# Modulation's sums over partitions: from one block of one-column products in the next mixer to ones matmuls inside the feed-forwards

## What is computed

```python
def second_block(x, c, ...):
    c_act = jax.nn.silu(c)
    mod = c_act @ ada_w[i] + ada_b[i]
    sh1, sc1, g1, sh2, sc2, g2 = [m[:, None, :] for m in jnp.split(mod, N_MOD, axis=-1)]
    h = rms_norm(x, mix_pre_g[i]) * (1.0 + sc1) + sh1
    y = hybrid_mixer(h, ...)
    x = x + g1 * rms_norm(y, mix_post_g[i])
    h = rms_norm(x, ffn_pre_g[i]) * (1.0 + sc2) + sh2
    y = swiglu_ffn(h, w_ffn_in[i], w_ffn_out[i])
    x = x + g2 * rms_norm(y, ffn_post_g[i])
```

## Time and profile before

| | |
|---|---|
| three runs | 1231.95, 1237.13 and 1238.58 us, median 1237.13 |
| the profiled execution | 1230.79 us, its span 1229.0 us |
| granted TensorE clock, mean | 0.983 |
| TensorE (PE) busy | 1163.5 us, 95% of the span |
| VectorE busy | 845.0 us, 69% |
| ScalarE busy | 614.6 us, 50% |
| the ada sums (lines 1554, 1557) | 24 and 168 operations, 8.3 and 81.5 us |
| the two old blocks on TensorE | 455.91 and 887.66 us after the span's start, 48 records each |

### The profile page before, as it was taken

How to read it: one execution, slowest core, us unless ns; L and a number is a source line. 1 busy time by engine, 2 the same in 40 slices (tenths; PEclk the granted TensorE clock), 3 DMA queues, 4 the chain that set the end, 5 groups by cost and what they waited for, 6 DMA issues and landing times.

```text
span 1229.0 us, 21102 instructions
## 1 busy us (share of the span) xinstructions
PE 1163.5 (95%) x9014; PEld 1127.7 (92%) x9014; DVE 845.0 (69%) x1270; ACT 614.6 (50%) x738; POOL 0.2 (0%) x4
## 2 busy tenths in 40 slices
PE   5899999999999999999999999999897988999996
PEld 5799899999999988998999999999897888999996
DVE  6995575777776788955657777767898647644443
ACT  7675336453434355753464534344577365434433
POOL 0000000000000000000000000000000000000000
PEclk9999999999999999999999999999998998999998
DMA  9455342756687653463427566876444221655501
GB/s 345 146 166 179 130 138 78 234 194 218 229 281 275 202 197 112 150 197 113 138 76 236 195 218 228 282 274 209 152 155 154 70 92 65 222 172 188 190 35 35
DMA packets 177614, 214.15 MB, mean 174 GB/s; under 512 B 3696, under 2 KB 160752, under 8 KB 177520
## 3 DMA queue, kind: packets, MB, share of 16 engines
q1 hardware_dynamic: 176800, 211.86, 52.3%
q10 hardware_dynamic: 720, 0.94, 0.2%
HBM read 211.74 MB, written 1.05 MB: 173 GB/s over the span
## 4 chain that ended last, share of the span: by engine, by line
PE 69%; DVE 19%; ACT 7%; issue 3%; DMA 1%; SPq 0%; DVEq 0%; ACTq 0%
PE stream L494 15%; PE stream L496 15%; PE stream L495 15%; DVE w_lo L1345 7%; PE steps L494 5%; PE steps L496 4%; PE steps L495 4%; ACT w_hi L914 3%; PE steps L829 2%; PE steps L684 1%; PE stream L705 1%; DMA raw<-in_w_in 1%; DVE conv_acc L1864 1%; ACT probs L914 1%; DVE score L1482 1%
## 5 line engine op out<-in xcount | busy, mean ns | idle before, releaser
L1345 DVE TENSOR_TENSOR w_lo<-raw,w_hi 128x2048 fp32r<-128x2048 f32 (+2 forms) x178 | 402.5, 2265 | 232.9 <-ACT w_hi L914 232.0
L914 ACT ACTIVATE w_hi<-raw 128x2048 fp32r<-128x2048 f32 (+2 forms) x178 | 336.5, 1893 | 336.6 <-PE stream L496 298.6
L494 PE MATMUL stream<-h_hi,w_hi 128*128 128x256 f32 x1576 | 451.2, 286 | 7.5 <-DVE h_lo L1737 3.8
L496 PE MATMUL stream<-h_hi,w_lo 128*128 128x256 f32 x1576 | 447.7, 284 | 0.0
L495 PE MATMUL stream<-h_lo,w_hi 128*128 128x256 f32 x1576 | 447.7, 284 | 0.0
L494 PEld LDWEIGHTS stream<-h_hi,w_hi 128*128 128x128 f32 x1576 | 303.9, 193 | 10.2 <-DVE w_lo L1345 5.2
L495 PEld LDWEIGHTS stream<-h_lo,w_hi 128*128 128x128 f32 x1576 | 303.9, 193 | 0.6 <-issue 0.5
L496 PEld LDWEIGHTS stream<-h_hi,w_lo 128*128 128x128 f32 x1576 | 303.7, 193 | 0.0
L494 PE MATMUL steps<-gu_hi,w_hi 128*128 128x256 f32 x528 | 149.8, 284 | 1.9 <-DVE gu_lo L1605 1.9
L496 PE MATMUL steps<-gu_hi,w_lo 128*128 128x256 f32 x528 | 149.7, 283 | 0.0
L495 PE MATMUL steps<-gu_lo,w_hi 128*128 128x256 f32 x528 | 149.7, 283 | 0.0
(11 more groups left out here) (289 smaller groups left out, 1635.0 us busy)
## 6 DMA issues: line engine op xcount, KB each, us to landing
raw<-in_w_ffn_in SPq DMA_DIRECT2D x66, 1024.0 KB, 5.2
raw<-in_w_in SPq DMA_DIRECT2D x54, 1024.0 KB, 5.8
raw<-in_w_ffn_out SPq DMA_DIRECT2D x33, 1024.0 KB, 7.1
ada_raw<-in_ada_w SPq DMA_DIRECT2D x24, 1024.0 KB, 5.4
raw<-in_w_out SPq DMA_DIRECT2D x8, 1024.0 KB, 5.1
raw<-in_w_proj_attn SPq DMA_DIRECT2D x8, 512.0 KB, 3.6
raw<-in_w_proj_hgrn SPq DMA_DIRECT2D x8, 512.0 KB, 4.6
raw<-in_w_o SPq DMA_DIRECT2D x4, 1024.0 KB, 5.0
```

Source lines behind the costliest of these rows:

```text
L494: pe.matmul(dst, w_h, x_h, start=start, stop=False, skip_group_check=True)
L496: return pe.matmul(dst, w_l, x_h, start=False, stop=stop, skip_group_check=True)
L914: return act.activation(out_, in_, func, **kw)
L1345: tt(wl[m % SPL][:, 0:n], raw[m % RAW][:, 0:n], wh[m % SPL][:, 0:n].bitcast(F32), ALU.subtract)\
```

## The change

The sum over partitions is taken by a matmul with a 128x128 matrix of ones as weights and the sums moving. ada_sum is split: ScalarE rounds a high part ada_h, VectorE subtracts the low part ada_l, both one step after the sum; another step later, behind up(i) and ahead of down(i - 1), TensorE multiplies ones with the high and the low part of 256 sums into bank S[3]. Every row of that bank then holds the 256 results. VectorE picks the diagonal: a multiply by the identity with a reduction (tensor_tensor_reduce) of each 128x128, giving one column of mod, then adds the bias. That is done behind gu_lo of the same step. Sums are made in steps 1 to 8 only, two each in steps 3, 5, 6 and 8, and their loads are due up to five units earlier; the eight groups follow in steps 3 to 10. ones is rounded to fp32r by ScalarE at the start of each of the two feed-forwards. ada_sum, ada_h and ada_l have four slots each. Bank S[3] is taken out of the round of gate and up units in these feed-forwards, which shifts the banks of all later units. Both old blocks, and VectorE's adds and gain operations beside them, are gone from the mixer and the second block; the gains are made at the end of the last group.

```diff
 ADA_LAYER = 12
-ADA_STEP = (1, 2, 3, 4, 5, 5, 6, 7, 8, 9, 9, 10)
+ADA_STEP = (1, 2, 3, 3, 4, 5, 5, 6, 6, 7, 8, 8)
+ADA_STEPS = sorted(set(ADA_STEP))
+ADA_GROUPS = [[j for j in range(ADA_LAYER) if ADA_STEP[j] == i] for i in ADA_STEPS]
 ADA_AFTER = {UFF[b] + n: ADA_LAYER * b + j for b in range(2)
-             for j, n in enumerate((3, 6, 11, 14, 17, 20, 23, 24, 26, 29, 32, 35))}
+             for j, n in enumerate((3, 6, 11, 14, 17, 19, 21, 24, 25, 27, 28, 30))}
...
     for u in UNITS:
+        if u[0] == "gate" and u[1] < 2 and u[2] == 0:
+            free_at.append(last[3])
+            last[3] = ("mod", len(ADA_GROUPS) * (u[1] + 1))
...
             for _ in range(2 if u[0] in ("merge", "tw") or shifted(u) else 1):
+                if bank == 3 and u[0] in ("gate", "up") and u[1] < 2:
+                    bank = 0
                 banks.append(bank)
...
-    ada_sum = at("ada_sum", [P, ADA_LAYER, UC], F32, 128)
+    ada_sum = at("ada_sum", [P, 4, UC], F32, 128)
+    ada_h = at("ada_sum_hi", [P, 4, UC], F32R, 132)
+    ada_l = at("ada_sum_lo", [P, 4, UC], F32R, 136)
+    mod_term = at("modulation_term", [P, 4, P], F32, 140)
...
+    ones_r = at("ones_r", [P, P], F32R, 142)
...
-        def modulation(b):
-
-            if b == 0:
-                for e, c in BANKS[ada_unit][1]:
-                    pe.wait_ge(evac[e], c)
-            pe.wait_ge(ada_summed, ADA_LAYER * (b + 1))
-            for j in range(2 * ADA_LAYER):
-                mm = pe.matmul(ada_bank[b][:, j:j + 1], ada_sum[:, j // 2, P * (j % 2):P * (j % 2) + P], ones[:, 0:1],
-                               start=True, stop=True)
-            mm.then_inc(ada_done, 1)
+        def modulation(b, g):
+
+            if g == 0:
+                pe.wait_ge(*ones_rounded.at(b))
+                pe.wait_ge(evac[MOD_FREE[b][0]], MOD_FREE[b][1])
+            if b or g:
+                pe.wait_ge(ada_read.sem, len(ADA_GROUPS) * b + g)
+            for n, j in enumerate(ADA_GROUPS[g]):
+                pe.wait_ge(ada_lo, ADA_LAYER * b + j + 1)
+                dst = S[3][:, UC * n:UC * n + UC]
+                pe.matmul(dst, ones_r, ada_h[:, j % 4, :], start=True, stop=False)
+                pe.matmul(dst, ones_r, ada_l[:, j % 4, :], start=False, stop=True).then_inc(ada_done, 1)
...
             stream(3)
-            stream(3 * FS - 5, normed(2 * b + 1))
+            stream(2, normed(2 * b + 1))
+            for i in range(2, FS):
+                if i - 2 in ADA_STEPS:
+                    modulation(b, ADA_STEPS.index(i - 2))
+                stream(3 if i < FS - 1 else 2)
...
             stream(1)
-            if b == 1:
-                modulation(0)
...
-        modulation(1)
         stream(7, normed(4))
...
         def feed_forward(b):
+            if b < 2:
+                f(ones_r, ones, ACT.Copy).then_inc(*lane.mark(ones_rounded))
...
+                if b < 2 and i - 1 in ADA_STEPS:
+                    for j in ADA_GROUPS[ADA_STEPS.index(i - 1)]:
+                        n = ADA_LAYER * b + j + 1
+                        act.wait_ge(ada_summed, n)
+                        if n > 4:
+                            act.wait_ge(ada_done, n - 4)
+                        f(ada_h[:, j % 4, :], ada_sum[:, j % 4, :], ACT.Copy).then_inc(ada_hi, 1)
...
+        def summed_low(b, g):
+
+            for j in ADA_GROUPS[g]:
+                n = ADA_LAYER * b + j + 1
+                dve.wait_ge(ada_hi, n)
+                if n > 4:
+                    dve.wait_ge(ada_done, n - 4)
+                tt(ada_l[:, j % 4, :], ada_sum[:, j % 4, :], ada_h[:, j % 4, :].bitcast(F32), ALU.subtract).then_inc(ada_lo, 1)
+                lane.last = (ada_lo, n)
...
+        def modulation(b, g):
+
+            first = 2 * (ADA_LAYER * b + ADA_GROUPS[g][0])
+            n = 2 * len(ADA_GROUPS[g])
+            dve.wait_ge(ada_done, ADA_LAYER * b + ADA_GROUPS[g][-1] + 1)
+            for c in range(n):
+                dve.tensor_tensor_reduce(mod_term[:, c, :], S[3][:, P * c:P * c + P], ident, 1.0, 0.0, ALU.mult,
+                                         ALU.add, flat_mod[:, first + c:first + c + 1]).then_inc(*lane.step())
+            dve.wait_ge(*lane.last)
+            cols = flat_mod[:, first:first + n]
+            tt(cols, cols, pc("ada_b", first, n), ALU.add).then_inc(*lane.mark(ada_read))
+
+        def gains(b):
+
+            dve.wait_ge(*lane.last)
...
+            ts_(gain[:, 1, :], mod[:, 4, :], 1.0, None, ALU.add).then_inc(*lane.step())
+            tt(gain[:, 2, :], mod[:, 2, :], pc("mix_post", 0, 8), ALU.mult).then_inc(*lane.step())
+            tt(gain[:, 3, :], mod[:, 5, :], pc("ffn_post", 0, 8), ALU.mult).then_inc(*lane.step())
+            dve.wait_ge(*lane.last)
+            tt(gain[:, 1, :], gain[:, 1, :], pc("ffn_pre", 0, 8), ALU.mult).then_inc(*lane.mark(gains_set))
...
+                if b < 2 and i - 2 in ADA_STEPS:
+                    modulation(b, ADA_STEPS.index(i - 2))
+                    if i - 2 == ADA_STEPS[-1]:
+                        gains(b)
+                if b < 2 and i - 1 in ADA_STEPS:
+                    summed_low(b, ADA_STEPS.index(i - 1))
                 for j in range(ADA_LAYER if b < 2 else 0):
                     if ADA_STEP[j] == i:
                         sum_ada(ADA_LAYER * b + j)
...
-                modulation(0)
-                dve.wait_ge(*lane.last)
-                ts_(gain[:, 0, :], mod[:, 1, :], 1.0, None, ALU.add).then_inc(*lane.step())
-                dve.wait_ge(*lane.last)
-                tt(gain[:, 0, :], gain[:, 0, :], pc("mix_pre", 0, 8), ALU.mult).then_inc(*lane.mark(gains_set))
...
         conv(range(1, 7), (0, 1))
-        modulation(1)
-        dve.wait_ge(*lane.last)
-        ts_(gain[:, 1, :], mod[:, 4, :], 1.0, None, ALU.add).then_inc(*lane.step())
-        tt(gain[:, 2, :], mod[:, 2, :], pc("mix_post", 0, 8), ALU.mult).then_inc(*lane.step())
-        tt(gain[:, 3, :], mod[:, 5, :], pc("ffn_post", 0, 8), ALU.mult).then_inc(*lane.step())
-        dve.wait_ge(*lane.last)
-        tt(gain[:, 1, :], gain[:, 1, :], pc("ffn_pre", 0, 8), ALU.mult).then_inc(*lane.mark(gains_set))
```

More of the change, by code:

```diff
@@ L152, in plan_banks @@
 def plan_banks():
-    count, bank, last, out = {"act": 0, "dve": 0, "gu": 0}, 0, {}, []
+    count, bank, last, out, free_at = {"act": 0, "dve": 0, "gu": 0}, 0, {}, [], []
     for u in UNITS:
+        if u[0] == "gate" and u[1] < 2 and u[2] == 0:
+            free_at.append(last[3])
+            last[3] = ("mod", len(ADA_GROUPS) * (u[1] + 1))
         e = evac_engine(u)
@@ L172, in plan_banks @@
         out.append((banks, free, count[e] if e else 0))
-    return out
-BANKS = plan_banks()
+    return out, free_at
+BANKS, MOD_FREE = plan_banks()
 def build(nc, a, out):
@@ L281, in build @@
     gain = small("gain2", [P, 4, KC])
+    flat_mod = mod.rearrange("p j c -> p (j c)")
+    ones_r = at("ones_r", [P, P], F32R, 142)
     rs_t = small("rstd_of_token", [P, NT])
@@ L354, in build @@
     x2_new = Event("x2_updated", 4)
[L355 to L358, removed]
+    ada_hi, ada_lo = sem("ada_hi"), sem("ada_lo")
+    ada_read = Event("modulation_read", len(ADA_GROUPS))
+    evac["mod"] = ada_read.sem
+    gains_set, ones_rounded = Event("gains_set"), Event("ones_rounded")
     sh_hi, sh_lo, v_sig, g_silu = (Event(n) for n in ("shift_hi", "shift_lo", "value_gate_set", "shifted_silu_set"))
@@ L537, in stream @@
                     pe.wait_ge(evac[e], c)
-                if m == ada_unit:
-                    pe.wait_ge(*ada_out.at(0, 0))
                 wait = dict(before or {})
@@ L863, in _ @@
         stream(1)
-        modulation(1)
         stream(7, normed(4))
         pe.wait_ge(*c_rows.at(0))
-        pe.wait_ge(*ada_out.at(0, 1))
         first = attend(2, 0, [evacuated(unit(2, "k1"))])
@@ L1277, in _ @@
         tick()
-        act.wait_ge(ada_done, 2)
+        act.wait_ge(ada_done, 2 * ADA_LAYER)
         f(qa[DH:DH + H], ident[DH:DH + H, DH:DH + H].unsqueeze(2).broadcast_to([H, H, T]), ACT.Copy).then_inc(*lane.step())
@@ L1429, in normalise @@
             low(3)
[L1431 to L1436, removed]
+        def summed_low(b, g):
[18 more added lines that the diff above has]
+            dve.wait_ge(*lane.last)
+            if b == 0:
+                ts_(gain[:, 0, :], mod[:, 1, :], 1.0, None, ALU.add).then_inc(*lane.step())
+                dve.wait_ge(*lane.last)
+                tt(gain[:, 0, :], gain[:, 0, :], pc("mix_pre", 0, 8), ALU.mult).then_inc(*lane.mark(gains_set))
+                return
+            ts_(gain[:, 1, :], mod[:, 4, :], 1.0, None, ALU.add).then_inc(*lane.step())
+            tt(gain[:, 2, :], mod[:, 2, :], pc("mix_post", 0, 8), ALU.mult).then_inc(*lane.step())
+            tt(gain[:, 3, :], mod[:, 5, :], pc("ffn_post", 0, 8), ALU.mult).then_inc(*lane.step())
+            dve.wait_ge(*lane.last)
+            tt(gain[:, 1, :], gain[:, 1, :], pc("ffn_pre", 0, 8), ALU.mult).then_inc(*lane.mark(gains_set))
         def rotate(x, n, cos, sin):
@@ L1552, in sum_ada @@
```

(10 more changed lines are left out.)

## The result

| | before | changed | ratio, 95% interval |
|---|---|---|---|
| median of 8 runs each | 1234.3 us (1231.95 to 1238.58) | 1226.32 us (1223.13 to 1229.7) | 0.9939, 0.992 to 0.9958 |
| the profiled execution | 1230.79 us, span 1229.0 | 1223.13 us, span 1221.4 | |
| granted TensorE clock, mean | 0.983 | 0.988 | |

The granted clock is given as a share: at 0.50 TensorE has 11 matmuls in 2.00 us (461 to 463 us), at 1.00 it has 20 in 2.00 us (182 to 184).

A forecast was written before the change was run, and what follows sets the result against it. Whichever of TensorE (feed-forwards) and VectorE (head of the second block) ends last at a place bounds it. Terms +5.8 - 1.4 - 6.7 - 3.7 - 0.65 = -6.65, say -6.7, took the median from 1237.1 to 1230.4 us, range 1223 to 1239.

The forecast's parts named there:

- 1, ones matmuls: Feed-forwards of both layers: 48 ones matmuls at 0.12 us each, all on the path: +5.8 us.
- 2, block in the mixer: Layer 1's mixer: removing the old block ends VectorE's losses of 5.77, 0.5 and 0.45 us: -6.7 us.
- 3, end of the first feed-forward: End of first feed-forward: without the last ada sum there, TensorE's wait of 1.34 us goes: -1.4 us.
- 4, end of the second: End of second feed-forward: split 2.4 us earlier, gap left about 1.1, clock staying up 1.3 more: -3.7 us.
- 5, block in the second block: Head of second block: TensorE's 5.25 us give nothing, VectorE loses five small operations: -0.65 us.
- 6, VectorE in the feed-forwards: Feed-forwards: VectorE's added work costs 0; t, the time per reduce, 0.35 us; step 6 slack 5.0 - 6t = 2.9 us.
- rival A: More comes back: slow clock at 611 to 613 us goes and TensorE's full 8.0 returns: -9.4 us; chance 0.14.
- rival C: Slower: reduces out of PSUM dear, TensorE waits at step 6 from t = 0.83 us; +9.3 at 1.226; chance 0.08.
- Rival B: Less comes: mixer gives only 4.2, second block's head 2.4, ones matmuls cost 7.1: -1.6 us; chance 0.28.

The follow-up runs named there:

- ones_doubled: Changed kernel with the pair of ones matmuls of each sum done twice: 1231.59 us, ratio to the kernel before 0.9979.
- steps_only: Kernel before with only the ada sums' steps and load times of the changed kernel, both old blocks kept: 1227.87 us, ratio to before 0.9958.
- reduces x2: Changed kernel with each diagonal reduce done twice: 1231.67 us, ratio to the kernel before 0.9979.
- x3: Changed kernel with each diagonal reduce done three times: 1245.03 us, ratio to the kernel before 1.0088.
- x6: Changed kernel with each diagonal reduce done six times: 1277.44 us, ratio to the kernel before 1.0341.
- no_block_in_mixer: Kernel before without TensorE's 24 one-column products in layer 1's mixer, VectorE's add kept: 1225.08 us, ratio to before 0.9941.

## Why the prediction was right, and where it was not

| part | forecast | measured | from |
|---|---|---|---|
| 1, ones matmuls | +5.8 | +5.76 | F0, F1 of ones_doubled against steps_only |
| 2, block in the mixer | -6.7 | -6.95 | M |
| 3, end of the first feed-forward | -1.4 | -1.56 | F0 of steps_only |
| 4, end of the second | -3.7 | -2.34, and -1.31 of clock | F1 of steps_only; H |
| 5, block in the second block | -0.65 | -0.67 | S |
| 6, VectorE in the feed-forwards | 0, slack 2.9 | +0.45, slack 0 | F0, F1 against steps_only, less part 1; reduces x2, x3, x6 |
| clock in N | not counted (rival A) | -1.37 in the first profile, +1.55 in the second, against before | N |

The six parts add up to -6.6 as measured, against -6.65; with N's -1.37 they are the -7.99 of the segments.

**Part 1** held: the stream's 0.12 us, by which 48 matmuls are 5.8 us; measured are 5.76, 0.120 each.

**Part 2** held by its own working. Its 8.0 us for TensorE stand in no row and were the author's estimate: the block's 7.06 us, and about 1 us for the slow clock behind it, at which the unit has 11 matmuls in 2.00 us where 20 are the pace at 1.00. In before the clock is 0.50 from 460 to 466 us; in no_block_in_mixer and in the changed kernel it is 1.00 over 455 to 470. TensorE's and ScalarE's side moved by 7.9 us (ScalarE's query squares, from 473.97 - 455.75 = 18.2 to 467.48 - 457.16 = 10.3 us behind the split), close to the 8.0, but only 6.95 arrived downstream, since VectorE ends last. The take-away run splits it into 6.45 for TensorE's products and 0.5 for VectorE's operations. The measured removal, 6.45 us, goes with the records' 0.109 to 0.147 each.

**Parts 3, 4 and 5** held within 0.2 us. Part 4's first term, 2.4, is 2.34. Its "about 1.1 us" for the gap left over does not follow from its own 2.67 less 2.4; measured are 0.32 in steps_only and 0.81 in the changed kernel. With either the clock stayed at 1.00 (873 to 876 us and 866 to 869), so the term came out. Its second, 1.3 of clock, came with every short gap ahead of the second block; but one of four long gaps kept the clock too, so it is what the long gap usually costs, not always.

**Part 6 is the step that failed**, though its term, 0, came out nearly, at 0.45. "That leaves 5.0 - 6t = 2.9 us of slack", and "from t = 5.0/6 = 0.83 us on TensorE waits" for rival C: the count started VectorE's step when up was done and left out 4.2 us of split in front of gu's product, whose release hangs on the same event. The true point is step 5, at t = (17.8 - 16.9)/4, about 0.22 (an estimate from that count), and the reduces take 0.24. The forecast of t, 0.35, was too high; with it and the right count TensorE would have been 0.5 us short in step 5. Two errors cancelled: that the term came out is luck. C's mechanism was real and much nearer than its chance of 0.08 by a threshold of 0.83: at t = 0.48 the gain is down to 0.9979, at 0.72 the kernel is slower.

**Rival A's** stretch at 611 to 613 did not come back in the first profile (604 to 610 at clock 1.00) and did in the second. It belongs to the execution and not to the change: the two profiles of the changed kernel have 165.11 and 168.03 us in N. Of the 7.7 us between the two profiled executions 1.37 are this stretch; the median over eight executions, which fall on either side of it, gives 7.5 by the ratio. **Rival B** fell: none of its lower bounds was met.

Left open: what decides in an execution whether the clock falls in N, or behind a long gap in H.

## What to carry to other kernels

Cost work by who ends last at its place: the same 48 small products were worth 6.45 us in one mixer and nothing in the next block, and the best version moves only the first. When you count the slack of an engine whose order is written out, start the step at the operation that really opens it, and look for a wait in front of it that hangs on the same event as your deadline. A change that costs nothing may have used up the slack: double the new work once to see how much is left. And look for short waits in the starts of TensorE's matmuls: those that decided here, up to 0.4 us, were in no list of waits.

## What the runs showed of the hardware that I had not expected

- A short wait costs TensorE more than its idle time in the records: 0.27 us more in each of three (0.97 for 0.71 shown, mean), and a loss of 0.41 showed no idle time at all.
- In layer 1's mixer the slow stretches of the clock come in whole steps of 1.4 to 1.5 us and vary between executions of one kernel: 165.1, 166.5 or 168.0 us for the same code. A segment that differs by such a step shows nothing of an edit.
